# The setup of a fused two-block kernel, by quarters of the features instead of halves

## The reference, cut to what matters

```python
mod_x = jnp.matmul(jax.nn.silu(c), w_mod[l]) + b_mod[l]          # c: 1 x 1024, w_mod: 1024 x 3072
mod_c = jnp.matmul(jax.nn.silu(c_ctx), w_mod[l]) + b_mod[l]
sh_x, sc_x, gt_x = mod_x[:, :D_MODEL], mod_x[:, D_MODEL:2 * D_MODEL], mod_x[:, 2 * D_MODEL:]
hx = rmsnorm(x, norm_g[l]) * (1.0 + sc_x[:, None, :]) + sh_x[:, None, :]     # x: 512 x 1024
hc = rmsnorm(ctx, norm_g[l]) * (1.0 + sc_c) + sh_c                           # ctx: 256 x 1024
z = jnp.matmul(h, w_in).astype(f32)      # aq, ak (256 each), av, ag (512 each), alr (32), ... of z
alog = jax.nn.log_sigmoid(jnp.einsum('btnr,nrk->btnk', alr, gla_up.astype(f32)) + gla_ub.astype(f32)) / GLA_TAU
# then, per chunk of 64 tokens, decays exp(cumsum(alog)) scale the queries and keys of the linear attention
```

## Time and profile before

| | us |
|---|---|
| median of 3 runs | 1315.31 (1314.8 to 1315.57) |
| profiled execution, span | 1313.0 |
| TensorE busy | 1266.9 (96%) |
| VectorE busy | 698.7 (53%) |
| ScalarE busy | 417.0 (32%) |
| GpSimd busy | 398.1 (30%) |

### The profile page before, as it was taken

The page is one execution under the profiler, slowest core; times in us unless marked ns, Lnnn a source line. Parts: engine busy times, 40 slices in busy tenths (PEclk is TensorE's granted clock), DMA queues, the critical chain, the costliest instruction groups (busy, mean ns, idle before and its releaser), DMA issues.

```text
span 1313.0 us, 24617 instructions
## 1 busy us (share of the span) xinstructions
PE 1266.9 (96%) x9971; PEld 772.5 (59%) x9971; DVE 698.7 (53%) x1422; ACT 417.0 (32%) x904; POOL 398.1 (30%) x470
## 2 busy tenths in 40 slices
PE   5999999999999999999999999999999999999997
PEld 3454655555656666687445885446645786455553
DVE  4356567847234444573473563247646373237745
ACT  4243213253433332101024002347613102236721
POOL 0100000202334443181432320225761250115671
PEclk9999999999999999999999999999999999999999
DMA  9710112011130100042426315110004415100001
GB/s 308 288 64 0 67 66 80 26 39 65 66 130 3 67 3 3 2 153 104 147 74 137 97 32 192 65 53 1 2 16 98 135 33 192 65 1 2 1 1 64
DMA packets 71535, 96.59 MB, mean 74 GB/s; under 512 B 27639, under 2 KB 35247, under 8 KB 71422
## 3 DMA queue, kind: packets, MB, share of 16 engines
q1 hardware_dynamic: 71050, 94.76, 21.7%
q10 hardware_dynamic: 372, 0.27, 0.1%
HBM read 92.89 MB, written 2.13 MB: 72 GB/s over the span
## 4 chain that ended last, share of the span: by engine, by line
PE 85%; DVE 6%; SPq 3%; ACT 3%; issue 1%; DMA 1%; POOL 0%; DVEq 0%; POOLq 0%; ACTq 0%
PE PS L147 81%; PE PS L2830 2%; DVE AR L2936 2%; ACT AR L3058 1%; SPq L187 1%; DMA bias_rows<-AR 1%; DVE AR L2923 1%; SPq L304 1%; SPq L308 1%; ACT AR L3068 0%; SPq L309 0%; SPq L312 0%; DVE AR L2106 0%; DVE AR L866 0%; PE PS L2164 0%
## 5 line engine op out<-in xcount | busy, mean ns | idle before, releaser
L147 PE MATMUL PS<-AR 64*64 64x64 f32 (+13 forms) x9334 | 1196.2, 326 | 21.8 <-ACT AR L3068 6.0
L147 PEld LDWEIGHTS PS<-AR 64*64 64x64 f32 (+5 forms) x9334 | 703.0, 152 | 485.1 <-issue 384.7
L3058 ACT ACTIVATE AR<-AR 128x257 f32<-128x257 f32 (+5 forms) x160 | 84.9, 531 | 96.1 <-DVE AR L2936 86.1
L2936 DVE CUSTOM_DVE_ANT_0 AR<-PS,AR 128x257 f32<-128x257 f32 (+5 forms) x160 | 72.2, 451 | 60.5 <-PE PS L147 43.0
L412 POOL TENSOR_TENSOR AR<-AR 128x1 f32<-128x1 f32 (+4 forms) x26 | 21.9, 841 | 258.6 <-DVE AR L407 211.8
L1189 DVE SCALAR_TENSOR_TENSOR AR<-AR 128x441 f32<-128x441 f32 (+2 forms) x96 | 78.6, 819 | 15.7 <-ACT AR L1146 12.0
L3119 POOL TENSOR_SCALAR AR<-AR 128x257 f32<-128x257 f32 (+5 forms) x96 | 53.4, 556 | 75.8 <-DVE AR L2942 70.3
L1612 DVE TENSOR_TENSOR AR<-PS,AR 128x256 f32<-128x256 f32 x60 | 25.5, 424 | 85.7 <-PE PS L147 82.4
L3117 POOL TENSOR_SCALAR AR<-AR 128x128 f32<-128x128 f32 (+3 forms) x64 | 39.0, 609 | 68.4 <-DVE AR L2942 64.5
L2053 POOL TENSOR_TENSOR AR<-AR 128x512 f32<-128x512 f32 x36 | 49.6, 1377 | 29.0 <-DMA AR<-in_w_o 26.0
L1738 ACT ACTIVATE AR<-PS 128x512 f32<-128x512 f32 x48 | 28.7, 597 | 82.5 <-PE PS L147 80.3
(11 more groups left out here) (264 smaller groups left out, 964.8 us busy)
## 6 DMA issues: line engine op xcount, KB each, us to landing
AR<-in_w_in SPq DMA_DIRECT2D x16, 2048.0 KB, 9.1
AR<-in_w_mod SPq DMA_DIRECT2D x6, 2048.0 KB, 13.1
AR<-in_w_out SPq DMA_DIRECT2D x4, 2048.0 KB, 13.0
AR<-in_x SPq DMA_DIRECT2D x8, 512.0 KB, 5.1
AR<-in_w_in SPq DMA_DIRECT2D x4, 1024.0 KB, 7.4
AR<-in_w_o SPq DMA_DIRECT2D x2, 2048.0 KB, 8.2
AR<-in_w_in SPq DMA_DIRECT2D x2, 1664.0 KB, 8.7
AR<-in_w_in SPq DMA_DIRECT2D x12, 256.0 KB, 4.2
```

What stands on the lines that cost most here:

```text
L147: return t.matmul(o, l, r, start=s, stop=p, skip_group_check=True)
L2936: v.do.tensor_tensor_reduce(PB[j % NJP][e][:, 0:nk], ps["s", l, j, e][:, 0:nk], bias_for(qb, kind, 2 * a + e, nk), 1.0, 3e38, ALU.add, ALU ...
L3058: a_.do.activation(P, P, ACT.Exp, bias=mn[:, j % NJS, e:e + 1], scale=-1.0, accum_out=su[:, j % NJS, e:e + 1]).then_inc(sa, na("p", l, j, e))
```

## The change

The loads of shift and scale come by quarters of the features (256 shift and 256 scale columns together, rows of 1 KB instead of 2 KB), and the query-and-key weights by quarters too; ctx is loaded after the first quarter; the upsampling weights `up` are zeroed at the end of `setup_g` (before: behind the barrier, in `gla_g`) and loaded in the setup. The transposes go by token tile. All first projections, the keys too, are summed by quarters of the features in banks that stay open (keys of x in banks 2 and 3, of ctx in bank 1, low-rank in 4 and 5, queries in 6 and 7), while bank 0 serves `mod` and `mod_turned`. The transposes of the decayed keys move from value tile 2 to value tile 4.

```diff
     def setup_s(s):
-        for i in range(2):
-            s.go.dma_start(xsv[:, i, :], I["ctx"][0, 128 * i:128 * i + 128, :]).then_inc(s_x[i], 16)
         aq, = wviews(1)
-        for half, ks in ((0, (0, 2)), (1, (1, 3))):
-            for k in ks:
-                s.go.dma_start(wmod[:, k], wm(512 * k)[0]).then_inc(s_wm[k], 16)
-            if half == 0:
+        for k in range(4):
+            for j in range(2):
+                s.go.dma_start(wmod[:, k, :, 256 * j:256 * j + 256], wm(1024 * j + 256 * k, 256)[0]).then_inc(s_wm[k], 16)
+            if k == 0:
                 load(s, 0)
-            sl = slice(4 * half, 4 * half + 4)
-            s.go.dma_start(aq[:, sl, :], wl[1][0][0][:, sl, :]).then_inc(s_ring[ring_slot(1)] if half else s_aq, 16)
+            sl = slice(2 * k, 2 * k + 2)
+            s.go.dma_start(aq[:, sl, :], wl[1][0][0][:, sl, :]).then_inc(s_aq[k] if k < 3 else s_ring[ring_slot(1)], 16)
+            if k == 0:
+                for i in range(2):
+                    s.go.dma_start(xsv[:, i, :], I["ctx"][0, 128 * i:128 * i + 128, :]).then_inc(s_x[i], 16)
+        s.wait_ge(sg, ng["up0"])
+        for n in range(2):
+            for r in (16 * n, 64 + 16 * n):
+                s.go.dma_start(up[r:r + 16, 256 * n:256 * n + 256], I["gla_up"][0, n]).then_inc(s_up, 16)
...
+    def turned_tokens(t, name, row, banks):
+        t.wait_ge(sv, nv["xn", row])
+        for i in range(2):
+            p = ps.take(t, name, row, i, bank=banks[i])
+            for m in range(4):
+                x = t.go.transpose(p[:, 128 * m:128 * m + 128], xsv[:, row, 512 * i + 128 * m:512 * i + 128 * m + 128], ident)
+            x.then_inc(st, nt(name, row, i))
     def setup_t(t):
+        for a in range(4):
+            turned_tokens(t, "hT", 2 + a, (2 * a, 2 * a + 1))
...
         mod(0)
+        t.wait_ge(s_oh, 32)
+        t.wait_ge(sv, nv["rt"])
+        for i, (k, lo, hi) in enumerate(BIAS):
+            p = ps.take(t, "brow", k, lo, bank=(3, 5, 6, 7)[i])
+            mm(t.go, p[0:13, 0:hi - lo], rt[0:33, 0:13], oh[0:33, 640 * k + lo:640 * k + hi], True, True).then_inc(st, nt("brow", k, lo))
+        mod_turned(0)
+        low_rank(t, 0, 256)
+        queries(t, 0, 0)
+        queries(t, 1, 0)
+        for a in range(2):
+            turned_tokens(t, "hC", a, (1, 0))
+        keys(t, 0, 256, 0)
+        mod(1)
+        low_rank(t, 0, 0)
+        keys(t, 0, 0, 0)
+        keys(t, 1, 0, 0)
+        mod_turned(1)
+        keys(t, 1, 256, 0)
+        low_rank(t, 1, 256)
+        low_rank(t, 1, 0)
+        queries(t, 0, 1)
+        queries(t, 1, 1)
+        keys(t, 0, 256, 1)
         mod(2)
+        keys(t, 0, 0, 1)
+        keys(t, 1, 0, 1)
         mod_turned(2)
+        keys(t, 1, 256, 1)
+        low_rank(t, 2, 256)
+        low_rank(t, 2, 0)
         mod(3)
+        queries(t, 0, 2)
+        queries(t, 1, 2)
         mod_turned(3)
+        keys(t, 0, 256, 2)
+        low_rank(t, 3, 256)
+        low_rank(t, 3, 0)
         nt.mark("at", "setup")
...
+    def keys(t, a, lo, k):
+        w = query_key_weights(t, k)
+        hx = features(t, lo, k)
+        b = 2 + a if lo else 1
+        p = ps.banks[b] if k or not lo and a else ps.take(t, "ak", a, lo, bank=b)
+        p = p if lo else p[:, 256 * a:256 * a + 256]
+        for t8 in (2 * k, 2 * k + 1):
+            x = mm(t.go, p, w[:, t8, 256 + 128 * a:384 + 128 * a], hx[:, t8, :], t8 == 0 and (lo > 0 or a == 0), t8 == 7)
...
     def setup_v(v):
+        v.wait_ge(sa, na["squares", 5])
+        rsq_v(v, rstd[:, 2:6], ss[:, 2:6], 1.0 / 1024, "x")
+        normed(2)
+        normed(3)
+        for a in range(4):
+            turned_tokens_v("hT", hT, 2 + a, a)
+            if a < 2:
+                normed(4 + a)
...
+        row(0)
+        turned(0)
+        modulated(0, hT, "hT", 0)
         v.wait_ge(sa, na["squares", 1])
         rsq_v(v, rstd[:, 0:2], ss[:, 0:2], 1.0 / 1024, "ctx")
+        for a in range(2):
+            normed(a)
+        for a in range(2):
+            turned_tokens_v("hC", hC, a, a)
+        modulated(0, hC, "hC", 8)
+        for k in range(1, 4):
+            row(k)
+            turned(k)
+            modulated(k, hT, "hT", 0)
+            modulated(k, hC, "hC", 8)
     def setup_a(a):
...
+        modulated(0, hT, "hT", 0)
+        for row in range(2):
+            squares(row)
...
     def gla_t(t):
-        low_rank(t, 1)
-        queries(t, 0, 4, 8)
-        ps.ring = list(range(7))
+        keys(t, 0, 0, 2)
+        keys(t, 1, 0, 2)
+        keys(t, 1, 256, 2)
+        ps.ring = [0, 4, 5]
...
-        queries(t, 1, 4, 8)
-        key(0)
-        key(1)
-        ps.ring = list(range(8))
+        for a in range(2):
+            queries(t, a, 3)
+        keys(t, 0, 256, 3)
+        for a in range(2):
+            keys(t, a, 0, 3)
+        keys(t, 1, 256, 3)
+        ps.k, ps.ring = 0, [0, 4, 5, 1, 2, 3, 6, 7]
         for a in range(6):
             p = ps.take(t, "av", a)
             projN(t, p, w, 0, 512, a, ("av", a))
-            if a == 2:
+            if a == 4:
                 for i in range(4):
                     gla_ends_t(t, 0, i)
     def gla_v(v):
         keys_of(0)
+        keys_of_context()
         gla_sums_v(v, 0)
+        keys_of(1)
         gla_sums_v(v, 1)
-        keys_of(1)
     def gla_a(a_):
-        query(0)
         a_.wait_ge(st, nt["bb"])
...
         a_.do.activation(u2, u2, ACT.Ln, bias=one_c, scale=1.0).then_inc(sa, na("softplus"))
+        query(0)
         query(1)
```

More of the change, by code:

```diff
@@ L287, in program @@
     s_wm = [landing(f"w_mod{k}") for k in range(4)]
[L288 removed]
+    s_up = landing("gla_up")
+    s_aq = [landing(f"gla_queries_keys{k}") for k in range(3)]
     s_x = [landing(f"x{i}") for i in range(6)]
     BIAS = [(k, lo, hi) for k in range(2) for lo, hi in ((0, 512), (512, 640))]
[L291 removed]
+    XC = ((256, 768), (0, 256))
     def setup_s(s):
@@ L322, in setup_t @@
         t.wait_ge(s_rl, 16)
-        p = ps.take(t, "rl")
+        p = ps.take(t, "rl", bank=2)
         t.go.transpose(p[0:32, 0:12], rl[0:12, 0:32], ident[0:12, 0:12]).then_inc(st, nt("rl"))
[L325 to L330, removed]
         def mod(k):
-            t.wait_ge(s_wm[k], 16)
-            p = ps.take(t, "mod", k, bank=k // 2 if k % 2 else None)
+            t.wait_ge(s_wm[k], 32)
+            p = ps.take(t, "mod", k, bank=0)
             for half in range(2):
@@ L395, in queries, with features @@
[L395 to L402, removed]
-            x.then_inc(st, nt("aq", a))
+    def features(t, lo, k):
+        hx, h = (hT, "hT") if lo else (hC, "hC")
+        for t8 in (2 * k, 2 * k + 1):
+            t.wait_ge(*((sa, na[h, t8]) if t8 % 2 else (sv, nv[h, t8])))
+        return hx
@@ new lines, in low_rank, with query_key_weights @@
+    def low_rank(t, k, lo):
+        w, = weights(t, 0)
+        hx, n = features(t, lo, k), 512 if lo else 256
+        b = 4 if lo else 5
+        p = ps.banks[b] if k else ps.take(t, "alr", lo, bank=b)
+        for q in range(2):
+            x = mm(t.go, p[64 * q:64 * q + 64, 0:n], w[:, 2 * k + q, :], hx[:, 2 * k + q, :], k == 0, k == 3)
+        if k == 3:
+            x.then_inc(st, nt("alr", lo))
+            nt.mark("weights", 0)
+    def query_key_weights(t, k):
+        if k < 3:
+            t.wait_ge(s_aq[k], 16)
+            return wviews(1)[0]
+        return weights(t, 1)[0]
@@ new lines, in queries @@
+    def queries(t, a, k):
+        w = query_key_weights(t, k)
+        hx = features(t, 256, k)
+        p = ps.banks[6 + a] if k else ps.take(t, "aq", a, bank=6 + a)
+        for t8 in (2 * k, 2 * k + 1):
+            x = mm(t.go, p[:, :], w[:, t8, 128 * a:128 * a + 128], hx[:, t8, :], t8 == 0, t8 == 7)
+        if k == 3:
+            x.then_inc(st, nt("aq", a))
+    def keys(t, a, lo, k):
+        w = query_key_weights(t, k)
+        hx = features(t, lo, k)
+        b = 2 + a if lo else 1
+        p = ps.banks[b] if k or not lo and a else ps.take(t, "ak", a, lo, bank=b)
+        p = p if lo else p[:, 256 * a:256 * a + 256]
+        for t8 in (2 * k, 2 * k + 1):
+            x = mm(t.go, p, w[:, t8, 256 + 128 * a:384 + 128 * a], hx[:, t8, :], t8 == 0 and (lo > 0 or a == 0), t8 == 7)
+        if k == 3:
+            x.then_inc(st, nt("ak", a, lo))
@@ L455, in setup_v @@
[L455 to L458, removed]
+            v.do.tensor_tensor(A_, pmv[:, :, 2:4], g_, ALU.mult).then_inc(sv, nv())
+            v.do.tensor_tensor(B_, pmv[:, :, 0:2], bm, ALU.add).then_inc(sv, nv())
+            v.do.tensor_tensor(A_, A_, bg_, ALU.add).then_inc(sv, nv("modAB", k))
@@ L463, in setup_v @@
[L463 to L476, removed]
@@ L499, in setup_a @@
             ps.empty(sa, na, "brow", k, lo)
[L500 to L510, removed]
-            for m in range(4 * half + 1, 4 * half + 4, 2):
-                a.do.activation(hT[:, m, :], hT[:, m, :], ACT.Identity, bias=modB[:, m:m + 1], scale=modA[:, m:m + 1]).then_inc(sa, na("hT", m))
-            for m in range(4 * half + 1, 4 * half + 4, 2):
```

(14 more changed lines are left out.)

117 lines of the change are left out of this document (45 added, 72 removed).

## The result

The changed kernel takes 1334.74 us (median of 4 executions, 1332.33 to 1335.66) against 1315.24 us before: a ratio of 1.0148 (95% interval 1.0134 to 1.0161), 19.5 us slower. The forecast was slower by 13.7, 1329.0, in a range of 1321 to 1334; the sign and the place were right, the size was too small. The profiled execution is the shortest of the four, 1332.33 us with a span of 1330.5, which is 17.5 more than the span of 1313.0 before.

A forecast was written before the change was run, and what follows sets the result against it. TensorE, busy for 96% of the span, was taken as the bound: state sums +11.9 us later, plus 1.8 for the clock, made +13.7, from 1315.3 to 1329.0 us, in a range of 1321 to 1334.

The forecast's parts named there:

- the stand: Ahead of the first state sums: TensorE idle 12.3 us, waiting for ScalarE's and VectorE's chain to value(5); bounds 9 and 13.
- Rival 3: Ahead of the state sums: the 12.3 us stand doesn't appear, G decides alone, 1312 or 1310 us; chance 0.04.
- rival 4: Start and state sums: new order does nothing, stand short by 3 us of slack, 1315 to 1316; chance 0.02.
- rival 1: Stand is there, but the start is quicker or the clock holds: G +2 to +5, 1322 to 1325; chance 0.14.
- rival 2: Projections: quarters also starve on modulation or ctx, 1 to 2 us three times, 1333 to 1336; chance 0.08.
- the start wins nothing: Setup through keys: projections by quarters win nothing, keys ending at 87.8 us against 87.5 before.
- G: Gain of the quarters at the end of the keys: -0.3 us, bounds -3 to +5.
- T0: Start of the first quarter's projections, the first low-rank matmul: 28.9 us against 32.91 before.
- the end of the keys: End of TensorE's query and key projections: 87.8 us, from T0 28.9 + 56.9 + 2.2 - 0.2.
- the clock behind the stand: At the state sums: TensorE falls to half clock after the stand, costing 1.8 us; bounds 0 and 2.2.
- I count no give-back: Behind the state sums: TensorE's work and order unchanged and still the bound, so no further term counted.
- the spread: Whole kernel: the same 2.3 us around the profiled span; a measurement tells 0.2%, 2.6 us, from no change.

The follow-up runs named there:

- values_early: Changed kernel with two copies earlier in their engines' lists: value(4) ahead of the second gla_queries_v, value(5) right behind value(3); 1329.23 us.
- late_keys: Changed kernel with keys of the last three quarters behind the bb matmuls and transposes of the decayed keys behind value tile 2; 1321.79 us.
- ends_at_2: Changed kernel with only the transposes of the decayed keys put back behind value tile 2; 1332.75 us.
- stand_filled: Changed kernel with 14 matmuls of unused result put ahead of the first state sums, where TensorE stands; 1331.49 us.
- before_ring: Kernel before the change, with the changed kernel's PSUM ring position at the end of the linear attention; 1316.74 us against 1314.94.
- ring_phase: Changed kernel with only the PSUM ring position at the end of the linear attention set back to bank 5 next; 1332.61 us.
- gate_first: Changed kernel with the whole first gate tile (8 matmuls) ahead of the first state sums instead of between the transposes behind them; 1334.42 us.
- gate_first_filled: gate_first with 6 matmuls of unused result in the rest of TensorE's stand ahead of the state sums; 1326.61 us.
- brow_first: late_keys with the ring position set back, plus vector transposes and bias-row matmuls ahead of the transposes of x; 1319.19 us.

## Why the prediction was right and wrong

**Right: the stand.** Forecast 12.3 us in front of the state sums, measured 12.39, by the chain that was named: transposes at 123.25, sums at 143.98, 20.73 us apart (20.7 forecast). values_early shows that the two copies end the wait, late_keys that it exists because keys were taken from behind `bb`, ends_at_2 that the move of the transposes is not its cause. Rival 3 (the stand doesn't appear) and rival 4 are out, and so is rival 1 (no fall of the clock). The measured 1334.74 lies in the band of rival 2 (1333 to 1336), but not by its mechanism: no wait of TensorE between 40 and 120 us is listed, and the one for ctx is 0.44 us.

**Right: the start wins nothing.** Forecast G = -0.3, measured -1.3. The two halves of that sum were each off, in opposite directions, so that it came out near is in part luck. T0 came at 27.86 instead of 28.9, because the scaled rows were ready at 15.1 and the transposes took 5.46 us instead of 6.0. But from T0 to the end of the keys it took 61.0 us instead of 58.9. The start was also less to win from than it seemed: the first 33 us of the kernel before hold 14.4 of the 46.1 us in which TensorE isn't busy, not most of them. Part of the 2.1 is the clock: it is at half already before T0 and until past 31.

```profile
27.00:30.00 3.00, 2.14 (x5) 0.50 1.09 357
30.00:33.00 3.00, 3.00 (x5) 0.63 1.08 357
```

The first twelve records take 6.82 us for 4.3 of work, 2.5 lost where 1.8 was counted. The other 1.4 us is in the long group behind 36.90, which shows no wait and a granted clock of 1.00; it lies ahead of `bb` (done at 80.4 instead of 79.2), and which matmuls are slower there stays open. The loads ran at 349 to 361 GB/s from 33 to 40 us, where the prediction took 373 for rows of 1 KB; no wait of TensorE comes of it.

**Right: the clock behind the stand.** 1.8 forecast, 2.07 measured in the profile (6.63 us instead of 4.56), 2.06 in stand_filled's, and 1.4 to 1.8 in its median.

**Wrong: "I count no give-back. Behind the sums TensorE's work and order are the same."** They are, but the banks aren't. This is the step that failed: `ps.k = 0` ahead of the values changes which bank every later `ps.take` gives, and one of the later places mixes ring banks with named ones. The term was put at nothing, and it measures 1.8 us: in before_ring's median, and in ring_phase's profile (its median moved by only 0.7). Without it the 1334.74 would be 1332.9 and inside the range. The edit stood in the diff, and the prediction only checked the banks of its own stage.

The terms together: 1.3 (end of keys) + 13.8 (value tiles moved ahead of the transposes) + 20.73 - 22.85 (from the transposes to the sums, after and before) = +12.95, + 2.07 (clock) + 1.8 (ring) = +16.8 of the profiled 17.5; of the rest, 0.5 comes in the last 70 us. The forecast had 11.9 + 1.8. So of the 5.8 us between the 13.7 forecast and the 19.5 measured, 1.8 are the ring, 1.1 the start of the state sums, 0.3 the clock, 0.7 stay open in the profile, and 2.0 lie between the profiled execution and the median.

**Also wrong: the spread.** The profiled execution is +17.0 against the median before, but the median over executions +19.5 (first measurement) and +18.5 (second). The prediction carried the last digit of one execution to the median, which holds for the kernel before (1314.8 to 1315.6) and not for all. Two things in the traces show how executions of the same code come apart. First, seven profiles (the changed kernel's two, ring_phase, values_early, stand_filled, gate_first, gate_first_filled) share their code up to the transposes of the decayed keys and reach these between 122.56 and 125.54 us: their first low-rank matmul comes between 27.65 and 29.40, and its group of twelve records takes 6.36 to 7.59 us, as the clock falls earlier or later. Second, before_ring's profile is of its longest execution, 3.0 us above its median: there the 28 records at 913.05 take 4.78 us instead of 3.34 in the kernel before, at a granted clock of 0.83 from 915 to 918 instead of 1.00, behind a wait that is as short as before (0.99 and 0.98 us). That the missing 1 to 2.4 us of the changed kernel are of these kinds is argued and not shown: both its profiles are of its shortest executions, and the mean granted clock of the four (0.989, 0.991, 0.988, 0.989) doesn't follow their times (1332.33, 1334.75, 1335.66, 1334.72).

No version here beats the kernel before; the nearest is brow_first with 1319.19. Its remaining 4 us lie ahead of the state sums (135.54 against 131.03). Two waits that the kernel before doesn't have, 1.6 us of `U` and 1.2 us of the transposes of the decayed keys, are 2.8 of these 4.5; the other 1.7 lie in the start and what the clock loses there.

## What to carry to other kernels

An earlier start of the busiest engine was worth nothing here, and the work that filled it was the cover of a chain further on: for each piece of work that is moved forward, ask which wait it stood beside. When a stage is rearranged, compare where it leaves every allocator (here the PSUM ring) and not only what it computes. Where the busiest engine must stand, look at its clock behind the stand before pricing a shorter one.

## What the runs showed of the hardware

Matmuls that nobody uses took time off a kernel: 14 of them, 12 us, 1.4 to 1.8 us by the medians and 2.06 in the profiled stretch; 6 of them, 5.2 us, 7.4 to 7.8 us by the medians and 5.1 in the profiled stretch. In both the state sums then ran at a granted clock of 1.00 where it was 0.50. A stand of 12.4 us was followed by one stretch at half clock (until about 149). A stand of 5.5 us with a half-idle stretch behind it (1.45 of 3 us busy) was followed by two, the second with 7 us of full work at 0.50; in one execution of four (1328.06, mean granted clock 0.993 against 0.987 and 0.988) probably less of it. The half-idle stretch without the stand (2.03 of 4 us busy, no wait over 0.7 us) was still followed by one, 0.51 from 151 to 154. The clock also fell ahead of T0 while TensorE was listed as busy, in the bias-row and two-column matmuls (0.85 from 24 to 26), so in this trace busy time alone didn't keep it up. The Trainium skill, "TensorE: Matmul & The Clock Gate" (What's actually happening), says that the clock depends on how busy the engine was lately; the trace agrees for the stands. Why it fell ahead of T0 no run here shows.
